# One program for the join and the feed-forward stage: the first feed-forward units behind the join's last product

## What is computed

```python
y = jnp.concatenate([y_a, y_b, y_c, y_d], axis=-1) @ w_out[l]
x = layer_norm(ALPHA * x + g1 * y, ln1_w[l], ln1_b[l])
x = layer_norm(ALPHA * x + g2 * swiglu(x * (1.0 + sc2) + sh2, w_ffn_in[l], w_ffn_out[l]), ln2_w[l], ln2_b[l])

def swiglu(h, w_in, w_out):
    g, u = jnp.split(h @ w_in, 2, axis=-1)
    return (jax.nn.silu(g) * u) @ w_out
```

## Time and profile before

| | before |
|---|---|
| median of 3 runs | 2263.49 us (2262.19 to 2265.18) |
| own time of the profiled execution | 2257.96 us |
| its span, first to last instruction | 2256.2 us |
| TensorE busy | 2104.8 us (93% of the span) |
| VectorE busy | 1262.5 us (56%) |
| ScalarE busy | 746.2 us (33%) |
| GpSimd busy | 432.4 us (19%) |
| mean granted clock of TensorE | 0.951 |

### The profile page before, as it was taken

The page is one execution under the profiler, slowest core; times in us unless marked ns, Lnnn a source line. Parts: engine busy times, 40 slices in busy tenths (PEclk is TensorE's granted clock), DMA queues, the critical chain, the costliest instruction groups (busy, mean ns, idle before and its releaser), DMA issues. The chain is left out here.

```text
span 2256.2 us, 27762 instructions
## 1 busy us (share of the span) xinstructions
PE 2104.8 (93%) x10549; PEld 1589.7 (70%) x10549; DVE 1262.5 (56%) x2133; ACT 746.2 (33%) x1380; POOL 432.4 (19%) x472
## 2 busy tenths in 40 slices
PE   6998999996969999999999999899999887989998
PEld 4744464485758888888888887765888764658876
DVE  6581795247873333223544323568999777762433
ACT  2222021144113322222444222456222243761415
POOL 2900001042310000000000000323666551300210
PEclk9999999955989999999999999899999998999999
DMA  8543110023233333235343332212211102003101
GB/s 324 157 136 109 39 57 1 1 76 122 64 107 92 93 93 97 84 96 158 117 120 112 91 99 85 76 48 57 71 47 51 36 1 76 1 30 133 44 1 75
DMA packets 195977, 184.83 MB, mean 82 GB/s; under 512 B 13246, under 2 KB 166142, under 8 KB 192538
## 3 DMA queue, kind: packets, MB, share of 16 engines
q1 hardware_dynamic: 192890, 172.85, 24.6%
q0 software_dynamic: 2880, 10.49, 1.3%
q10 hardware_dynamic: 96, 0.02, 0.0%
HBM read 169.37 MB, written 12.64 MB: 81 GB/s over the span
## 5 line engine op out<-in xcount | busy, mean ns | idle before, releaser
L1835 DVE TENSOR_TENSOR ff_part<-ff_raw,ff_part 128x1024 fp32r<-128x1024 f32 (+2 forms) x152 | 164.9, 1085 | 435.8 <-ACT ff_part L1743 435.8
L1743 ACT ACTIVATE ff_part<-ff_raw 128x1024 fp32r<-128x1024 f32 (+2 forms) x152 | 144.0, 948 | 433.7 <-PE ps L1633 431.7
L1631 PE MATMUL ps<-h,ff_part 128*128 128x512 f32 x704 | 275.8, 392 | 4.2 <-DVE ff_part L1835 4.2
L1632 PE MATMUL ps<-h,ff_part 128*128 128x512 f32 x704 | 275.0, 391 | 0.0
L1633 PE MATMUL ps<-h,ff_part 128*128 128x512 f32 x704 | 274.9, 390 | 0.0
L2451 DVE TENSOR_SCALAR_CACHE_REDUCE pj_junk<-NM,prm 128x384 uint8<-128x384 f32 (+1 forms) x186 | 163.7, 943 | 1.1
L1631 PEld LDWEIGHTS ps<-h,ff_part 128*128 128x128 f32 x704 | 132.8, 189 | 31.9 <-DVE ff_part L1835 4.6
L1631 PE MATMUL ps<-pj_part,h 128*128 128x512 f32 x384 | 153.1, 399 | 0.2 <-ACT PJ L2308 0.2
L1633 PEld LDWEIGHTS ps<-h,ff_part 128*128 128x128 f32 x704 | 132.8, 189 | 27.9
L1632 PEld LDWEIGHTS ps<-h,ff_part 128*128 128x128 f32 x704 | 132.9, 189 | 27.4
L1632 PE MATMUL ps<-pj_part,h 128*128 128x512 f32 x384 | 150.3, 392 | 0.0
(11 more groups left out here) (595 smaller groups left out, 4023.1 us busy)
## 6 DMA issues: line engine op xcount, KB each, us to landing
ff_raw<-in_w_ffn_in SPq DMA_DIRECT2D x88, 512.0 KB, 3.7
s_wm<-in_w_mod SPq DMA_DIRECT2D x16, 1024.0 KB, 4.9
pj_raw<-in_w_in SPq DMA_DIRECT2D x64, 256.0 KB, 2.6
ff_raw<-in_w_ffn_out SPq DMA_DIRECT2D x32, 384.0 KB, 3.4
ff_raw<-in_w_ffn_out SPq DMA_DIRECT2D x32, 320.0 KB, 3.0
mod_w<-in_w_mod SPq DMA_DIRECT2D x8, 1024.0 KB, 9.3
mod_x<-in_x SPq DMA_DIRECT2D x8, 512.0 KB, 14.5
mx_spread<-mx_lfd SPq DMA_DIRECT2D x16, 256.0 KB, 3.4
```

The costliest lines, as they stand in the source:

```text
L1631: nc.tensor.matmul(out, w[0], x[0], start=first, stop=False)
L1632: nc.tensor.matmul(out, w[0], x[1], start=False, stop=False)
L1743: nc.scalar.activation(part[s % 2][0][:, 0:n, :], raw[s][:, 0:n, :], ACT.Copy).then_inc(hi, 1)
L1835: v.tensor_tensor(part[s % 2][1][:, 0:n, :], raw[s][:, 0:n, :], part[s % 2][0][:, 0:n, :].bitcast(F32), ALU.subtract).then_inc(lo, 1)
```

## The change

The two stages become one block, `stage_join_ffn`. `stage_join` turns into `join_programs`, which returns the engine programs instead of running them; each engine of the new block first runs its join part and goes on with its feed-forward part. The barrier at the join's end, the clear behind it and the second barrier are gone. Instead `retire` clears the semaphores of earlier stages at the start of GpSimd's programs of the mixers (3 instructions), of the join (2) and of first_end (4).

The first two units of the feed-forward stage are issued beside the join's last tile. Their weights have buffers of their own, at the addresses of `jn_x` buffers that the join is through with, and the low part is written over the raw one. The intermediate buffers are placed elsewhere in the on-chip memory:

```diff
-    hid = [K.at(f"ff_hid{n}", 24 + 44 * n, [P, NF, HALF], FR) for n in range(2)]
-    raw = [K.at(f"ff_raw{s}", 112 + 4 * s, [P, KT, P]) for s in range(NR)]
-    part = [[K.at(f"ff_part{s}{n}", 8 * s + 4 * n, [P, KT, P], FR) for n in range(2)] for s in range(2)]
-    sil = [K.at(f"ff_sil{s}", 16 + 2 * s, [P, HALF]) for s in range(2)]
+    J = join_programs(K)
+    hid = [K.at(f"ff_hid{n}", 36 + 44 * n, [P, NF, HALF], FR) for n in range(2)]
+    raw = [K.at(f"ff_raw{s}", kb, [P, KT, P]) for s, kb in enumerate((12, 16, 8, 124))]
+    part = [[K.at(f"ff_part{s}{n}", 24 * s + 4 * n, [P, KT, P], FR) for n in range(2)] for s in range(2)]
+    raw_first = [K.at(f"ff_rawf{s}", kb, [P, KT, P]) for s, kb in enumerate((112, 104))]
+    low_first = [K.at(f"ff_lowf{s}", kb, [P, KT, P], FR) for s, kb in enumerate((112, 104))]
+    sil = [K.at(f"ff_sil{s}", 32 + 2 * s, [P, HALF]) for s in range(2)]
```

The waits of SP's first loads (J.x is the join's semaphore x), and TensorE's:

```diff
                     for s in range(NR):
+                        dst = raw[s]
                         if h or not first(r):
                             sp.wait_ge(lo, unit(h, r, NR) + s - (NR - 1))
-                        sp.dma_start(raw[s][:], ...
+                        elif s < 2:
+                            dst = raw_first[s]
+                            sp.wait_ge(J.x1r, NT - 2 + s)
+                        elif s == 2:
+                            sp.wait_ge(J.mev, NT)
+                        else:
+                            sp.wait_ge(J.stored[0], 16 * NT // 2)
+                        if not h and isinstance(r, int) and r == 1:
+                            sp.wait_ge(J.hr, NT)
+                        sp.dma_start(dst[:], ...
...
+                            if not h and first(r):
+                                pe.wait_ge(J.mev, NT - 1 + j)
+                            ws = part[s % 2]
+                            if not h and first(r) and j == 0:
+                                ws = [part[s][0], low_first[s]]
                             pe.wait_ge(lo, u + 1)
```

In the join's last tile (its x1 goes to `t_last`, in the place of `w_out_lo`) ScalarE splits unit 0 once tile 6 is multiplied and unit 1 once tile 7 is:

```diff
+            if i == NT - 1:
+                act.wait_ge(mm, NT - 1)
+                early(0)
+                act.wait_ge(mm, NT)
+                early(1)
             act.wait_ge(sq, 2 * i + 1)
```

More of the change, by code:

```diff
@@ L1472, in stage_join @@
     mm, mev, sq, x1r, hr, tr, thi, tev, chain = (K.sem("jn_" + n) for n in "mm mev sq x1r hr tr thi tev chain".split())
-    wl, yhi, ylo = (K.sem("jn_" + n) for n in "wl yhi ylo".split())
+    wl, yhi, ylo, g2_tr, g2_ev = (K.sem("jn_" + n) for n in "wl yhi ylo g2tr g2ev".split())
+    K.g2 = K.prm[:, 32:32 + KT]
     stored = [K.sem(f"jn_st{s}") for s in range(2)]
[L1475 to L1508, removed]
-                for k in range(KT):
[L1510 to L1605, removed]
@@ new lines, in tensor, with turn, parts @@
+    def tensor(pe):
+        def turn(i):
+            pe.wait_ge(hr, i + 1)
+            pe.wait_ge(g2_ev, 1)
+            if i >= 2:
+                pe.wait_ge(tev, 2 * (i - 1))
+            for k in range(KT):
+                last = nc.tensor.transpose(K.bank[4 + 2 * (i % 2) + k // 4][:, (k % 4) * P:(k % 4 + 1) * P],
+                                           h[i % 4][:, k * P:(k + 1) * P], K.ident[:])
+            last.then_inc(tr, 1)
+        pe.wait_ge(K.mod_in, 32)
+        for k in range(KT):
+            last = nc.tensor.transpose(K.bank[4 + k // 4][:, (k % 4) * P:(k % 4 + 1) * P], K.MOD[:, 5 * D + k * P:5 * D + (k + 1) * P], K.ident[:])
+        last.then_inc(g2_tr, 1)
+        for i in range(NT):
+            t = slice(i * P, (i + 1) * P)
+            if i >= 2:
+                pe.wait_ge(mev, i - 1)
+            def parts(k, b):
+                n = slice(b * HALF, (b + 1) * HALF)
+                low = y6_low[:, k, t] if k < 6 else yd_low[:, k - 6, t]
+                return K.bank[2 * (i % 2) + b][:], (yh[i % 2][:, k, :], low), (K.wo_high[k][:, n], wo_low[:, k, n])
+            if i == 0:
+                pe.wait_ge(yhi, 2)
+                for p, (yp, wp) in enumerate(((0, 0), (0, 1), (1, 0))):
+                    if p == 2:
+                        pe.wait_ge(ylo, 2)
+                    for k in range(KT):
+                        if p < 2:
+                            pe.wait_ge((K.wo_split, wl)[p], k + 1)
+                        for b in range(2):
+                            o, y, w = parts(k, b)
+                            last = nc.tensor.matmul(o, y[yp], w[wp], start=(p == 0 and k == 0), stop=(p == 2 and k == KT - 1))
+            else:
+                pe.wait_ge(ylo, 2 * i + 2)
+                for k in range(KT):
+                    for b in range(2):
+                        last = product(nc, *parts(k, b), k == 0, k == KT - 1)
+            last.then_inc(mm, 1)
+            if 1 <= i <= NT // 2:
+                turn(i - 1)
@@ L1764, in hidden @@
                         for a in range(2):
-                            split(u + a, 2 * j + a, KT, arrivals(h, 0, r))
+                            if h or j or not first(r):
+                                split(u + a, 2 * j + a, KT, arrivals(h, 0, r))
+                        if not h and j == 0 and isinstance(r, int) and r == 2:
+                            act.wait_ge(J.stored[1], 16 * NT // 2)
                         if j or not first(r):
@@ L1850, in hidden @@
                         for a in range(2):
-                            split(u + a, 2 * j + a, KT)
+                            if h or not first(r) or u + a == 3:
+                                split(u + a, 2 * j + a, KT)
                         if j or not first(r):
@@ L1877, in _ @@
         def _(pe):
-            for k in range(KT):
-                last = nc.tensor.transpose(K.bank[4 + k // 4][:, (k % 4) * P:(k % 4 + 1) * P], K.MOD[:, 5 * D + k * P:5 * D + (k + 1) * P], K.ident[:])
-            last.then_inc(g2_tr, 1)
+            J.tensor(pe)
             def back(i):
```

135 lines of the change are left out of this document (122 added, 13 removed).

## The result

| | before | after |
|---|---|---|
| median of 4 runs each | 2262.84 us | 2239.09 us (2235.16 to 2240.74) |
| ratio to before, 95% | | 0.9892 (0.9875 to 0.991) |
| five more runs, with 19 of before beside them | 2261.26 us | 2239.04 us, 0.9905 (0.9888 to 0.9921) |
| own time of the profiled execution | 2257.96 us | 2240.74 us |

The kernel is faster by 1.1%. By the medians of the first row, taken side by side, the gain is 23.75 us, with an interval from 20.4 to 28.3.

What follows compares the result with a forecast made beforehand. TensorE, busy 93% of the span, was taken to bound the kernel; 18.66 us of pause plus 2.94 of restart gave 21.6, and 2263.49 - 21.6 = 2241.9 us. Range: 2239.5 to 2248.

Steps and rivals of the forecast that it cites:

- the pause: Between the join's last matmul and the feed-forward stage: TensorE's idle time, of which the change saves 18.66 us.
- the restart: First feed-forward unit after the hole: slow matmuls at clock 0.50, costing 2.94 us that the change saves.
- more is won: Rival: TensorE works 1 us earlier in the join, its clock may rise sooner; 2239.5 to 2241 us, chance 0.08.
- Unit 0: First 24 feed-forward matmuls: start at 654.36 after VectorE's subtraction, some 0.6 us of waiting remaining at the boundary.
- Unit 2's split: VectorE's subtraction for the third feed-forward unit, behind the norm: in time by 0.2 to 0.8 us, the tightest point.
- Unit 3's split: VectorE's subtraction for the fourth feed-forward unit, behind h: ends at 668.8, slack 1.9 us.
- unit 4: Fifth feed-forward unit: load waits for the last h, takes 5 us; split ends at 674.9, slack at least 1.2 us.
- What was taken as free: g2 transposes moved before the join's first product, starting it 0.9 us later, and nine new GpSimd clears: cost 0.
- The clock fell: Rival: the 0.6 us wait at the boundary still lowers the clock; gain 18.7, 2244.8 us, chance 0.07.
- the long stretch without a pause: Slower rival: through join and feed-forward the chip answers unbroken TensorE work with clock 0.50; 2270 us, chance 0.04.
- The second pair late: Rival: unit 1's load lands late, unit 2 starts 5.8 us late; 2243 to 2248 us, 0.14 shared with unit 4.
- doesn't do what it says: Rival: an early split is held up on its engine until the norm is through, pause stays; about 2262 us, 0.03.

Runs made afterwards that it cites:

- the 26: Kernel before, unchanged, run 26 further times beside the experiments: median 2261.3 us, range 2256.2 to 2265.84.
- experiment 2: Changed kernel with VectorE's split of unit 2 behind the last h: 2240.03 us; changed kernel with load 1 held until the last tile's eviction: 2244.42 us.
- the repetition: Changed kernel timed again with no edit, five runs: 2239.04 us.
- the restart alone: Kernel before with 60 extra matmuls, results unread, keeping TensorE at work in the pause before the feed-forward stage: 2258.17 us, 0.9992.
- the late load: Changed kernel with the load of unit 1 held back until the last join tile is evicted: 2244.42 us, 0.9928.

## Why the prediction was right in its sum and wrong in its base

**The sum holds.** All nine runs of the changed kernel (mean 2238.8) against all thirty of before (the four beside the result and the 26, mean 2260.8) give a difference of 22.0 us, with a standard error of 0.9. The prediction had 21.6: 18.66 of the pause and 2.94 of the restart; the traces show 18.65 and 2.95. That the whole kernel agrees to 0.4 us is partly luck: the runs fix it to 1.9 us only, and a loss of 1.5 us in first_end and project could hide in that.

**The step that failed is the last one**, "the median of the runs is 5.53 above that execution, so I predict 2263.49 - 21.6", and with it the range, in which this base had no error. 2263.49 was the median of three runs that spanned 3 us, and all thirty runs put it at 2261.4, 2.1 lower. The profiled execution with 2257.96 lay 3.4 below that median, so neither of the two numbers stood for the kernel, and a distance of 5.5 us between them was a sign of a scatter that the range should have held. From 2261.4 the same sum gives 2239.8; the measured median is 2239.09. The scatter worked on both sides of the difference: beside the result the kernel before ran at 2262.84, only 0.65 below the base, and the other 2.15 of the 2.8 us are a gain of 23.75 us in those four runs of each kernel, which the later runs do not repeat (22.2). The lower end of 2239.5 was reasoned from mechanisms alone ("more is won"), and the base got no term. A mean of three runs with a deviation of 2.5 is uncertain by 2.5 / 1.73 = 1.4 us; that much more at both ends would have taken the result in.

**The steps at the boundary.** The join ended 1.98 us later in the trace of after (655.53 against 653.55), so 1.98 is taken off here. Unit 0 started at 654.37 (forecast 654.36). Load 1 was issued at 650.60 (650.6), ScalarE copied it at 655.20 (655.0 to 655.6), its split ended at 657.53 (657.4 to 658.0), unit 1 started at 659.93 (659.81; unit 0 took 5.56 us and not 5.45). Unit 2's split ended at 664.52 (664.5 to 665.1) and it started at 665.37 (665.26): a slack of 0.85 us where 0.2 to 0.8 were forecast, at the upper end since load 1 landed early in its bounds. The two kernels of experiment 2 confirm it with 0.9 and 0.7. Unit 3's split ended at 668.05 (668.8): 668.8 was reckoned from the late bound of h (667.6), and h ended at 666.92, near the early one (667.0). For unit 4 the rows are

```profile
673.05 1.06 ACT L1789 ACTIVATE ff_part<-ff_raw 128x1024 fp32r<-128x1024 f32 x1 [1.01 <-PE ps L1663]
674.14 1.23 DVE L1886 TENSOR_TENSOR ff_part<-ff_raw,ff_part 128x1024 fp32r<-128x1024 f32 x1 [1.38 <-ACT ff_part L1789]
```

ScalarE waits for the pair, which unit 2 has to leave (PE ps), and not for the load: the 5 us of landing that I had put there did not matter, and the split ends at 673.39 (674.9).

**What was taken as free was free.** The product at the join's start began 0.4 us later than in before, counted from the block's start (556.93 - 555.29 = 1.64, before 556.05 - 554.82 = 1.23), not 0.9, and in the repetition the second tile starts at the same distance as in before. The nine clears:

```profile
L124 POOLq EVENT_SEMAPHORE_RANGE_CLEAR  x9: 44/92/370, 222.2 to 1383.6; - x9
```

44 to 370 ns each, where 807 were the bound from the earlier trace rows; the bound had come from the one clear of before, which stands behind a barrier. In the join GpSimd's first low part starts 1.26 us behind the block's start, as in before: the two clears do not push it at all, where 0.4 us were forecast. The prediction called itself wrong if the stages from the mixers on grow: the mixers did not (333.2 us in both traces), first_end and project did, and why stays open.

**The rivals.** The clock fell behind none of the gaps of 0.8 to 1.0 us at the boundary (six traces, matmuls 0.23 us from start to start behind each). Nothing answers the long stretch without a pause: 807 us at 1.00. "The second pair late" and "doesn't do what it says" did not occur. "More is won" had its reason in a clock that rises sooner in the join; the trace of after shows it rising later there, and the repetition has the second tile at the old distance, so this was not the cause, although the time fell next to that case's bounds.

## What to carry to other kernels

A boundary between two stages costs the idle time of the busiest engine, from its last work in one to its first in the next; read it there and ask what of the next stage needs nothing of the last tile. Here most came from splitting the first three units of the next stage beside the last tile on the helping engines, and less than half from the barriers, the clear and the late load together. Rebuild the new order with old durations, and check the tightest slack by an experiment that moves it; here 0.2 to 0.8 us were forecast and 0.7 to 0.9 found. Give the base of a forecast its own error: with three runs and one trace it was off by 2.1 us, and the restart that was argued over is 2.94.

## What was not expected of the hardware

The clock can fall after a wait is over: in the run of the restart alone TensorE waited 2.72 us, went on at 1.00 for 1.2 us, and only then ran at 0.50 for 3.4 us. After the wait of 0.43 us at the new boundary, and after those of 1.76 and 1.30 us with the late load, it stayed at 1.00.

Clearing a range of semaphores took 44 to 370 ns at the starts of GpSimd's programs, and 807 ns behind the barrier in the earlier trace rows. Why they differ is not shown.

Executions of the same instructions differ by 2.6 us in one stage of 179 us, the longer one at the lower granted clock (0.93 against 0.95), and by up to 10 us in the whole kernel.
